# Two transformer blocks on one core: a rounding and split ahead of the gate's eviction, head sums one unit later, and six products of zeros for three

## The chip, the cores and the metric

The kernel runs on one core of a Trainium2 chip. The metric is the device time of one execution in microseconds (us), as the median of several runs. TensorE multiplies (its weight loads are listed apart, as PEld), VectorE (DVE) and ScalarE (ACT) do the element-wise work, GpSimd (POOL) helps, and SyncE (SP) issues the transfers. The engines run side by side, each takes its instructions in order, and they wait for each other by semaphores.

## The reference, cut to what matters

One token sequence of T = 256 positions with D = 1024 features, float32, runs through a first model of two layers ("stage a0", "a1"), and then through a second model of two layers ("b0", "b1"). A layer of the first model is, cut short:

```
xn   = rms_norm(h); proj = xn @ w_in            # q k v, index, conv, recurrence z, three gates
y_a  = attention over the top 64 keys; y_b = short conv * gate
y_c  = rwkv7(z):  kk = k*k_k;  kk *= rsqrt(sum over a head of kk*kk)      # "head sums of the keys"
       y = scan over time(...)
       yn = (y-mean)*rsqrt(var+eps)*ln_w + ln_b   # group norm, per head
       y_c = (yn + bonus) * g
mixed = sum over the three branches of sigmoid(gate_i) * (y_i @ w_branch_i)
h += mixed @ w_out;  h += conv_glu_ffn(rms_norm(h))
```

All products of activations with the large weights must have more than the accuracy of one rounded product, which is why each weight and each activation is split in two parts (below). The group norm and the head sums are the places that the change touches.

## The kernel before, in words

**Slabs and units.** The weights stream in as slabs of 128 x 2048 float32 (1 MB), one per unit of work; `UNITS_A` (line 44) lists the units of a layer of the first model in order. Those named here are w 0 and w 1 (the first two), rz 0 to 6 (the recurrence's inputs), uc, cb (convolution), ga, gb, gc 0 to 3 (the gates of the three branches), br0, br1, br2 (the branches' projections), out, up and down. Every unit makes three products for each weight tile (`gemm`, lines 1488 to 1490): high weight by high input, high by low, low by high. Before a unit can run, ScalarE must round its slab into `w_high` (step "round", `act_round`, line 594) and VectorE must subtract to get `w_low` (step "split", `dve_split`, line 967). There are three slab buffers and three pairs of high and low parts. A round waits for the slab's transfer and for the products of the unit three back; SyncE's next transfer into a slab waits for its split.

**Order of the work.** A list of steps is built once per stage by `schedule_a` and `woven`, and every engine walks the same list in order and does its own part of each step (`walk`). `woven` puts at unit u the round and split of the unit two ahead, then a "begin" (the first half of the unit's products) with the steps that stand amid the unit, then the unit's remaining products and its eviction, and then the steps put after it. A unit in `late` gets its round and split after the eviction instead. So the order of two steps in the list is their order in each engine's queue; an engine that has no part in a step passes over it.

**The group norm.** For gc 2 the list of before reads: begin, gn 1, unit, round and split of br2 0, gn 2. In gn 1 TensorE sums the squares per head (`head_sums`, line 1890), ScalarE takes the root (line 921, recorded like all calls of its helper under line 670) and VectorE the reciprocal (1369). In the unit ScalarE waits for the products of gc 2 and applies two sigmoids from the bank (767, also recorded under 670); they need another activation table than the root, so a table load of ScalarE lies between. In gn 2 TensorE spreads the reciprocal over the features (1901) and makes the factor g (2049); VectorE scales, adds and multiplies in two halves (1374, 1380, 1383), ScalarE makes the high part, and VectorE the low part (1101). Unit br2 0 multiplies these parts; it follows gc 3.

**The head sums of the keys.** After rz 3 GpSimd makes kk (2106), after rz 4 ScalarE squares it (864), after rz 5 TensorE sums per head (`kk_sum`, 1906, products at 1890) and VectorE clamps the sum (1287), and after rz 6 ScalarE takes the root (868) and the first attention scores are made (TensorE 1829, VectorE 1248, ScalarE exponentials 815). The sums' bank is read by the clamp only; the root is used again three units on.

**The start.** `pe_warm` multiplies zeros into a bank that nothing reads, as soon as GpSimd has set them, while the first transfers run. A product of float32 operands appears as two records of 128 x 512. TensorE's first real work is w 0 (24 products, lines 1776 to 1778), in whose first half two halves of slab 0 are waited for (`split_half`, line 978).

Of the kernel before, what the change touches and what calls it, by code (L numbers as in the profile page):

```python
# [355 lines left out]
def lead_steps(first):  # L356

    halves = [[("scaled", 2 * n), ("scaled", 2 * n + 1)] for n in range(2)]
    if first:
        steps = [("angles", 0)]  # L360
        for n in range(2):
            steps += [("scaled", n), ("round_half", n), ("split_half", n)]
        return (steps + [("angles", 1), ("angles", 2)] + halves[1] + [("round", 1), ("split", 1)]
                + [("square", i) for i in range(4)] + [("root_table", 0), ("gather", 0)])
    steps = []
    for n in range(2):
        steps += [("add", 2 * n), ("add", 2 * n + 1)] + halves[n] + [("square", 2 * n), ("square", 2 * n + 1)]
    return steps + [("gather", 0), ("split", 1)]


def woven(units, first, lead, after, mid, last=False, early=(), late=()):


    steps, rounded, n, done = list(lead), 2, len(units), set()

    def ready(u):
        nonlocal rounded
        out = []
        if rounded == u:
            out.append(("round", u))  # L380
            rounded += 1
        if u not in done:
            out.append(("split", u))
        done.add(u)
        return out

    for u in range(n):
        ahead = u + PARTS - 1
        split_next = ready(ahead) if ahead < n + (not last) else [] if last else [("round", ahead)]
        if units[u] not in late:  # L390
            steps += split_next
        if units[u] in mid:
            steps += [("begin", u)] + mid[units[u]]
        if units[u] in early:
            steps.append(("round", rounded))
            rounded += 1
        steps.append(("unit", u))
        if units[u] in late:
            steps += split_next
        for step in after.get(units[u], []):  # L400
            if step == ROUND_NEXT:
                if rounded < n:
                    steps.append(("round", rounded))
                    rounded += 1
            elif step == SPLIT_NEXT:
                steps.append(("split", u + PARTS))
                done.add(u + PARTS)
            else:
                steps.append(step)
    return steps  # L410


def schedule_a(first):
    after, mid = {}, {}

    def put(unit, *steps):
        after.setdefault(unit, []).extend(steps)

    def amid(unit, *steps):
        mid.setdefault(unit, []).extend(steps)  # L420

    amid(("w", 1), ("sum", 0), ("norm", 0), ("tables", 0))
    put(("w", 1), ("norm_x", 0))
    put(("ki", 0), ("params", 0), ("highs", 0), ("lows", 0))
    amid(("q", 0), ("ki_turn", 0))
    put(("q", 1), ("turns", 0), ("turns", 1))
    amid(("rz", 0), ("isc", 0), ("isc", 1))
    amid(("rz", 1), ("isc", 2), ("isc", 3))
    put(("rz", 2), ("turns", 2), ("turns", 3))
    for part in range(4):  # L430
        put(("rz", 1 + part), ("topk", part))
    put(("rz", 3), ("kk", 0))
    put(("rz", 4), ("kk_square", 0))
    put(("rz", 5), ("kk_sum", 0))
    put(("rz", 6), ("kk_root", 0))
    hosts = [("rz", 6)] + [("uc", i) for i in range(4)] + [("cb", 0), ("cb", 1)]
    for n, unit in enumerate(hosts):
        put(unit, *([("conv", n - 1)] if 1 <= n < 5 else []), *([("lora_inputs", 0)] if n == 2 else []))
        work = [(name, n - lag) for name, lag in (("pv", 3), ("turn", 2), ("scores", 0)) if 0 <= n - lag < 4]
        put(unit, *(work + [ROUND_NEXT] if unit == ("uc", 3) else [ROUND_NEXT] + work))  # L440
    amid(("uc", 3), ("lora", 0), ("kk_inverse", 0))
    put(("uc", 3), ("kk_spread", 0), ("kk_scale", 0), ("blend", 0), ("decay", 0), ("blended", 0))
    put(("cb", 0), ("keys", 0))
    put(("ga", 0), ("chunk", 0), ("mask", 0), ("chunk", 1), ("mask", 1))
    put(("ga", 1), ("chunk", 2), ("mask", 2), ("chunk", 3), ("mask", 3), ("blocks_out", 0), ("tok", 0), ("keys", 1), ("clear", 0),
        ("blocks_turn", 0))
    put(("ga", 2), ("invert", 0), ("tok", 1), ("post", 0), ("post", 1))
    put(("ga", 3), ("tok", 2))
    put(("gb", 0), ("off_diag", 0), ("bonus_shift", 0))
    put(("gb", 2), ("blocks_in", 0))  # L450
    put(("gb", 3), ("solve", 0))
    amid(("br0", 0), ("solve", 1))
    put(("br0", 0), ("solve", 2))
    amid(("br0", 1), ("solve", 3))
    put(("br0", 1), ("scan_rhs", 0))
    for c, unit in enumerate((("br1", 0), ("br1", 1), ("gc", 0), ("gc", 1))):
        amid(unit, ("scan_sa", c))
        put(unit, ("scan_y", c), *([("scan_rhs", c + 1)] if c < NCH - 1 else [("gn", 0), ("root_table", 0)]))
    amid(("gc", 2), ("gn", 1))
    put(("gc", 2), ("gn", 2))  # L460
    amid(("br2", 1), ("mix", 0))
    for i in range(4):
        if i < 3:
            amid(("out", i + 1), ("x_ffn", i))
            put(("out", i + 1), ("square", 4 + i))
    put(("out", 3), ("gather", 1), ("x_ffn", 3), ("square", 7), ("sum", 1))
    amid(("up", 0), ("sum", 2), ("norm", 1))
    put(("up", 0), ("spread", 1))
    put(("up", FT - 1), ("ffn", FT), ("ffn", FT + 1))
    put(("down", FT // 2 - 2), ("root_table", 0))  # L470
    return woven(UNITS_A, first, lead_steps(first), after, mid, early=[("br2", 0), ("br2", 1)],
                 late=[("gc", 2), ("br2", 1)])


def schedule_b(first):
# [38 lines left out]
    put(("out", 1), ("merge", 3))  # L514
    put(("out", 2), ("root_table", 0))
    return woven(UNITS_B, False, lead_steps(False), after, mid, not first)


SCHEDULE = {"a0": schedule_a(True), "a1": schedule_a(False), "b0": schedule_b(True), "b1": schedule_b(False)}


# [122 lines left out]
def flat(core, at, n=1):  # L644
    return core.ar[:, at * T:(at + n) * T]
# [1412 lines left out]
def pe_warm(core, eng):  # L2058

    eng.wait_ge(*core.sem("idle_set").next(eng))  # L2060
    for _ in range(3):
        eng.matmul(core.bank[6][:], flat(core, IDLE_)[:, 0:P], flat(core, IDLE_, 2), start=True, stop=True, skip_group_check=True)


def tensor_program(core, eng):
    banks = Banks(core, eng)
    pe_warm(core, eng)
    for stage in STAGES[:-1]:
        core.enter(stage)
        (tensor_a if stage[0] == "a" else tensor_b)(core, eng, banks, stage)  # L2070
    core.enter("end")
    add_up = pe_square(core, eng, banks, 4)
    for i in (1, 3, 2):
        add_up(i)
    pe_spread(core, eng, banks, "final_norm", 4)
# [855 lines left out]
```

How the kernel before makes its waits and increments, by code:

```python
    def at_least(self, eng, n):  # L117
        if n > 0:
            eng.wait_ge(self.sem, self.base + n)
# [14 lines left out]
    def settled(self):  # L134
        if self.last:
            self.eng.wait_ge(*self.last)
# [403 lines left out]
def sync_program(core, eng):  # L540
# [1 line left out]
    eng.dma_start(core.gains[:], d["gains"]).then_inc(sem("gains_in").sem, 16)  # L542
    for i in range(4):
        eng.dma_start(core.h[:, 2 * i:2 * i + 2, :], d["x_t"][:, 2 * i:2 * i + 2, :]).then_inc(sem(f"x_in{i}").sem, 16)
    slab_to(core, eng, 1)
    eng.dma_start(core.cc[:], d["common"]).then_inc(sem("const_in").sem, 16)
    slab_to(core, eng, 2)
    eng.dma_start(core.cm[:], d["const_a"]).then_inc(sem("model_in").sem, 16)
    eng.dma_start(core.vec[:], d["vec_a"][0]).then_inc(sem("vec_in").sem, 16)
    eng.dma_start(core.lora[:], d["lora"][0]).then_inc(sem("lora_in").sem, 16)
    for u in range(SLABS, SLABS_IN_ALL):
        eng.wait_ge(sem("slab_split").sem, u - SLABS + 1)
        slab_to(core, eng, u)
        if u == FIRST_SLAB["a1"] + SLABS:
            for name in ("convolved", "g_made"):
                eng.wait_ge(sem(name).sem, START["a1"][name])
            eng.dma_start(core.vec[:], d["vec_a"][1]).then_inc(sem("vec_in").sem, 16)
            eng.dma_start(core.lora[:], d["lora"][1]).then_inc(sem("lora_in").sem, 16)
        if u == FIRST_SLAB["b0"] - 20:
            eng.dma_start(core.cb[:], d["const_b"]).then_inc(sem("const_b_in").sem, 16)
    eng.wait_ge(sem("slab_split").sem, SLABS_IN_ALL)
    for i in range(4):
```

## Time and profile before

| | |
|---|---|
| median of 3 runs | 1680.03 us (1679.94 to 1680.36) |
| profiled execution | 1679.88 us, span 1678.1 us |
| TensorE busy | 1660.4 us, 99% of the span |
| weight loads | 1478.3 us, 88% |
| VectorE busy | 1196.9 us, 71% |
| ScalarE busy | 964.0 us, 57% |
| GpSimd busy | 211.7 us, 13% |
| transfers | 268.17 MB, mean 160 GB/s |
| granted TensorE clock, mean | 0.996 of full speed |

The span runs from the first to the last instruction, and the execution's time is 1.8 us longer. Busy time of TensorE counts overlapping products once, and the end of a product is modelled; so a pause shows best from the start of one product to the start of the next. A wait in the lists stands as "who <- what released it". Where the releaser is not seen it is written "issue".

### The profile page before, as it was taken

To read this page: it belongs to the slowest core of one execution; us is meant where nothing else is said; L and a number is where in the kernel's file an instruction comes from. 1 tells how busy PE (TensorE), PEld (TensorE's weight loads), DVE (VectorE), ACT (ScalarE), POOL (GpSimd) and SP (SyncE) were. 2 spreads that over 40 slices of the span, in tenths; PEclk is the share of its full clock that TensorE was granted. 3 is DMA by queue.
4 is the path that set the end of the run, shared out by engine and by line. 5 is a ranking of instruction groups with operands and counts; after the bars stand their busy time and mean duration, and the time that the engine had idled before them with its cause. 6 is when DMAs were issued, how large, how long until landed. Compare 5 with 4: busy or idle time off the path is not lost.

```text
span 1678.1 us, 29746 instructions
## 1 busy us (share of the span) xinstructions
PE 1660.4 (99%) x12378; PEld 1478.3 (88%) x12378; DVE 1196.9 (71%) x1676; ACT 964.0 (57%) x1459; POOL 211.7 (13%) x208
## 2 busy tenths in 40 slices
PE   8999999999999999999999999999999999999998
PEld 6999999999998999999999998778888987788887
DVE  7877446798888975538898875767766647667664
ACT  7674424655567564335555555665774556657743
POOL 1764400000001945200000000000000100000000
PEclk9999999999999999999999999999999999999999
DMA  7443522544545424424455454344344453443451
GB/s 266 147 152 119 178 102 101 201 179 176 185 179 184 173 101 142 155 102 175 152 183 199 176 201 176 129 148 174 128 175 177 169 199 135 150 162 141 163 188 51
DMA packets 48197, 268.17 MB, mean 160 GB/s; under 512 B 13568, under 2 KB 14464, under 8 KB 16448
## 3 DMA queue, kind: packets, MB, share of 16 engines
q1 hardware_dynamic: 38160, 263.65, 43.7%
q10 hardware_dynamic: 9136, 1.58, 0.5%
q8 instruction: 98, 1.61, 0.4%
q0 software_dynamic: 768, 1.05, 0.3%
q14 instruction: 35, 0.29, 0.0%
HBM read 264.42 MB, written 1.84 MB: 159 GB/s over the span
## 4 chain that ended last, share of the span: by engine, by line
PE 94%; DVE 3%; ACT 2%; issue 1%; DMA 0%; DVEq 0%; SPq 0%; ACTq 0%
PE bank L1488 12%; PE bank L1489 11%; PE bank L1490 11%; PE bank L2647 11%; PE bank L2649 10%; PE bank L2648 10%; PE bank L1541 8%; PE bank L1543 4%; PE bank L2677 2%; PE bank L2665 1%; DVE w_low L967 1%; PE bank L1937 1%; PE bank L1776 1%; ACT w_high L594 1%; PE bank L1778 1%; PE bank L1777 1%
## 5 line engine op out<-in xcount | busy, mean ns | idle before, releaser
L967 DVE TENSOR_TENSOR w_low<-slab,w_high 128x2048 fp32r<-128x2048 f32 x249 | 579.9, 2338 | 207.0 <-ACT w_high L594 199.7
L594 ACT ACTIVATE w_high<-slab 128x2048 fp32r<-128x2048 f32 x249 | 470.2, 1895 | 139.6 <-PE bank L2649 97.2
L1488 PE MATMUL bank<-act,w_high 128*128 128x256 f32 (+1 forms) x1744 | 503.1, 288 | 5.8 <-DVE act L1101 4.4
L1489 PE MATMUL bank<-act,w_high 128*128 128x256 f32 (+1 forms) x1744 | 493.9, 283 | 0.0
L1490 PE MATMUL bank<-act,w_low 128*128 128x256 f32 (+1 forms) x1744 | 493.7, 283 | 0.0
L1488 PEld LDWEIGHTS bank<-act,w_high 128*128 128x128 f32 (+1 forms) x1744 | 333.4, 191 | 17.1 <-issue 11.2
L1489 PEld LDWEIGHTS bank<-act,w_high 128*128 128x128 f32 (+1 forms) x1744 | 333.7, 191 | 0.9 <-issue 0.5
L1490 PEld LDWEIGHTS bank<-act,w_low 128*128 128x128 f32 (+1 forms) x1744 | 333.7, 191 | 0.1
L2647 PE MATMUL bank<-w_high,act 128*128 128x512 f32 x768 | 305.3, 398 | 0.0
L2649 PE MATMUL bank<-w_low,act 128*128 128x512 f32 x768 | 299.8, 390 | 0.0
L2648 PE MATMUL bank<-w_high,act 128*128 128x512 f32 x768 | 299.1, 389 | 0.0
L1541 PE MATMUL bank<-act,w_high 128*128 128x512 f32 x576 | 204.4, 399 | 0.0
L2202 POOL TENSOR_TENSOR arena<-arena 128x512 f32<-128x512 f32 x8 | 14.4, 1797 | 1297.7 <-ACT arena L619 1297.7
L2649 PEld LDWEIGHTS bank<-w_low,act 128*128 128x128 f32 x768 | 144.1, 188 | 31.0
L2647 PEld LDWEIGHTS bank<-w_high,act 128*128 128x128 f32 x768 | 144.3, 188 | 29.4 <-issue 1.3
L2648 PEld LDWEIGHTS bank<-w_high,act 128*128 128x128 f32 x768 | 144.5, 188 | 28.2
L670 ACT ACTIVATE arena<-bank 128x512 f32<-128x512 f32 (+3 forms) x134 | 70.1, 535 | 162.0 <-PE bank L1543 44.8
L1543 PE MATMUL bank<-act,w_low 128*128 128x256 f32 x576 | 161.8, 281 | 0.0
L1541 PEld LDWEIGHTS bank<-act,w_high 128*128 128x128 f32 x576 | 108.3, 188 | 26.1
L1543 PEld LDWEIGHTS bank<-act,w_low 128*128 128x128 f32 x576 | 108.9, 189 | 0.0
L2275 ACT ACTIVATE arena<-bank,small 128x512 f32<-128x512 f32 x80 | 54.8, 685 | 79.9 <-PE bank L2649 78.8
L1137 DVE SCALAR_TENSOR_TENSOR arena<-arena,vectors 128x255 f32<-128x255 f32 (+1 forms) x176 | 85.1, 483 | 12.4 <-ACT arena L670 3.6
(261 smaller groups left out, 1853.8 us busy)
## 6 DMA issues: line engine op xcount, KB each, us to landing
slab<-stream_a SPq DMA_DIRECT2D x143, 1024.0 KB, 4.8
slab<-stream_b SPq DMA_DIRECT2D x104, 1024.0 KB, 4.8
residual<-x_t SPq DMA_DIRECT2D x4, 256.0 KB, 6.0
slab<-stream_a ACTq DMA_DIRECT2D x2, 512.0 KB, 5.6
lora_weights<-lora SPq DMA_DIRECT2D x2, 512.0 KB, 7.7
out_t<-residual SPq DMA_DIRECT2D x4, 256.0 KB, 2.3
d_inverse<-arena POOLq DMA_DIRECT2D x2, 256.0 KB, 3.4
constants<-common SPq DMA_DIRECT2D x1, 384.0 KB, 8.8
```

The costliest lines, as they stand in the source:

```text
L594: line.did(eng.activation(core.wh[u % PARTS][:, 0:SLAB_WIDTH[u]], core.slab[u % SLABS][:, 0:SLAB_WIDTH[u]], ACT.Copy), core.sem("slab_high"))
L670: line.did(eng.activation(out, in_, func, **kw), tally)
L967: line.did(line.eng.tensor_tensor(core.wl[u % PARTS][:, 0:SLAB_WIDTH[u]], core.slab[u % SLABS][:, 0:SLAB_WIDTH[u]], core.wh[u % PARTS][:, ...
L1137: did(stt(out=out[:, lag:T], in0=src[:, 0:T - lag], scalar=col("conv", 2 * FT * tap + half * FT + j), in1=out[:, lag:T], op0=ALU.mult, op1 ...
L1488: eng.matmul(out, wh, xh, start=first, stop=False, skip_group_check=True)
L1489: eng.matmul(out, wh, xl, start=False, stop=False, skip_group_check=True)
L1490: return eng.matmul(out, wl, xh, start=False, stop=last, skip_group_check=True)
L1541: eng.matmul(out[:].rearrange("p (n t) -> p n t", n=2), wh[:, k, j, :], core.x[:, :, at, :], start=k == 0, stop=False, skip_group_check=True)
L1543: return eng.matmul(out[:, 0:T], wl[:, k, j, :], core.xh[:, at, :], start=False, stop=k == 7, skip_group_check=True)
L2647: mm(bank[b][:], high, wh[:, k, :], start=(half == 0 and k == 0), stop=False, skip_group_check=True)
L2648: mm(bank[b][:], low, wh[:, k, :], start=False, stop=False, skip_group_check=True)
L2649: last = mm(bank[b][:], high, wl[:, k, :], start=False, stop=(half == 1 and k == 3), skip_group_check=True)
```

## The change

Three edits. In `woven`, a unit named in `behind_mid` gets the round and split of the unit two ahead behind the steps amid it and ahead of its own eviction; gc 2 is named there and is in `late` no more. So at gc 2 the list reads: begin, gn 1, round and split of br2 0, unit, gn 2. The step `kk_sum` moves from behind rz 5 to behind rz 6, ahead of `kk_root`. `pe_warm` makes six products in place of three. Both layers of the first model have the first two edits; the third is at the start of the kernel alone.

```diff
-def woven(units, first, lead, after, mid, last=False, early=(), late=()):
+def woven(units, first, lead, after, mid, last=False, early=(), late=(), behind_mid=()):
...
-        if units[u] not in late:
+        if units[u] not in late and units[u] not in behind_mid:
             steps += split_next
         if units[u] in mid:
             steps += [("begin", u)] + mid[units[u]]
+        if units[u] in behind_mid:
+            steps += split_next
...
-    put(("rz", 5), ("kk_sum", 0))
-    put(("rz", 6), ("kk_root", 0))
+    put(("rz", 6), ("kk_sum", 0), ("kk_root", 0))
...
     return woven(UNITS_A, first, lead_steps(first), after, mid, early=[("br2", 0), ("br2", 1)],
-                 late=[("gc", 2), ("br2", 1)])
+                 late=[("br2", 1)], behind_mid=[("gc", 2)])
...
-    for _ in range(3):
+    for _ in range(6):
         eng.matmul(core.bank[6][:], flat(core, IDLE_)[:, 0:P], flat(core, IDLE_, 2), start=True, stop=True, skip_group_check=True)
```

## Rows read from the trace of the kernel before

**Rows 1.** The page: the chain that ended last, shares of the span by engine.

```profile
PE 94%; DVE 3%; ACT 2%; issue 1%; DMA 0%; DVEq 0%; SPq 0%; ACTq 0%
```

**Rows 2.** Waits of the whole span, TensorE only: total us, times, longest us.

```profile
PE bank L1488 <- DVE act L1101: 4.4, 2, 2.2
...
PE bank L1890 <- issue: 1.0, 2, 0.5
```

**Rows 3.** Timeline of TensorE, layer 0: start us, us, engine line op; idle time in brackets.

```profile
271.57 0.28 PE L1489 MATMUL bank<-act,w_high 128*128 128x256 f32 x1
271.69 0.28 PE L1490 MATMUL bank<-act,w_low 128*128 128x256 f32 x1
274.16 0.36 PE L1488 MATMUL bank<-act,w_high 128*128 128x256 f32 x1 [2.19 <-DVE act L1101]
```

**Rows 4.** Timeline of ScalarE, layer 0, around the group norm.

```profile
260.87 1.28 ACT L670 ACT_TABLE_LOAD   x1 [0.16 <-ACT arena L670]
263.27 0.84 ACT L670 ACTIVATE arena<-bank,vectors 128x256 f32<-128x256 f32 x2 [1.12 <-PE bank L1490]
264.00 1.91 ACT L594 ACTIVATE w_high<-slab 128x2048 fp32r<-128x2048 f32 x1
```

**Rows 5.** Timeline of VectorE, layer 0, around the group norm.

```profile
260.79 1.75 DVE L1369 RECIPROCAL arena<-arena 128x256 f32<-128x256 f32 x1 [8.16 <-ACTq L141]
265.94 2.29 DVE L967 TENSOR_TENSOR w_low<-slab,w_high 128x2048 fp32r<-128x2048 f32 x1 [3.40 <-ACT w_high L594]
268.15 0.68 DVE L1374 TENSOR_TENSOR arena<-bank,arena 128x512 f32<-128x512 f32 x1
...
273.32 1.30 DVE L1101 TENSOR_TENSOR act<-arena,act 128x512 fp32r<-128x512 f32 x2
```

**Rows 6.** Timeline of TensorE, layer 0, head sums of the keys.

```profile
76.97 0.28 PE L1490 MATMUL bank<-act,w_low 128*128 128x256 f32 x1
77.77 0.64 PE L1890 MATMUL bank<-arena,constants_a 128*32 128x256 f32 x8 [0.52 <-issue]
78.33 0.38 PE L1488 MATMUL bank<-act,w_high 128*128 128x256 f32 x1
```

**Rows 7.** Timeline of TensorE, layer 0, eight like products, for the group norm (L1890).

```profile
259.32 0.28 PE L1490 MATMUL bank<-act,w_low 128*128 128x256 f32 x1
...
260.10 0.38 PE L1488 MATMUL bank<-act,w_high 128*128 128x256 f32 x1
```

**Rows 8.** Timeline of ScalarE, layer 0, from the square of the keys on.

```profile
76.61 1.06 ACT L670 ACTIVATE arena<-arena 128x1024 f32<-128x1024 f32 x1 [4.47 <-POOL arena L2106]
...
87.11 1.28 ACT L670 ACT_TABLE_LOAD   x1
88.84 0.40 ACT L670 ACTIVATE arena<-arena,small 128x128 f32<-128x128 f32 x1 [0.44 <-DVE small L1254]
```

**Rows 9.** Timeline of VectorE, layer 0, same stretch.

```profile
83.31 0.41 DVE L1287 TENSOR_SCALAR arena<-bank 128x256 f32<-128x256 f32 x1
...
86.54 0.96 DVE L1248 SCALAR_TENSOR_TENSOR arena<-bank,arena 128x768 f32<-128x768 f32 x1
```

**Rows 10.** Timeline of TensorE, layer 0, first transpose of scores.

```profile
97.79 0.82 PE L1841 MATMUL bank<-constants,arena 128*128 128x128 f32 x6
```

**Rows 11.** Timeline of all engines, start of the kernel.

```profile
1.32 4.87 PE L2062 MATMUL bank<-arena 128*128 128x512 f32 x6 [1.32 <-POOL arena L2211]
...
8.84 0.80 PE L1776 MATMUL bank<-w_high,act 128*128 128x512 f32 x1 [2.65 <-DVE w_low L978]
...
14.26 2.29 DVE L967 TENSOR_TENSOR w_low<-slab,w_high 128x2048 fp32r<-128x2048 f32 x1 [0.85 <-ACT w_high L594]
...
16.60 0.50 PE L1776 MATMUL bank<-w_high,act 128*128 128x512 f32 x1 [0.45 <-DVE w_low L967]
```

**Rows 12.** Busy time by stretch: PE, PEld, DVE, ACT, POOL; granted clock, DMA share, GB/s.

```profile
271.00:274.00 3.00, 0.97 (x9) 0.76 (x7) 2.71 (x6) 1.08 (x3) 0.00 (x0) 1.00 0.49 208
8.84:12.35 3.51, 3.51 (x9) 2.80 (x9) 3.36 (x17) 3.48 (x8) 0.00 (x0) 0.51 0.99 407
```


## The prediction

> **What bounds the kernel now.** I read the page's chain of waits first, then the waits of TensorE alone, then the timelines of the three places that the change touches, engine by engine. The chain lies on TensorE for 94% of the span [rows 1], so an edit pays only where TensorE itself stops or does less. The list of its waits has two entries in places that are touched: 4.4 us in two stops ahead of products of L1488, released by L1101 on VectorE, and 1.0 us in two stops at L1890 [rows 2]. There are two layers, hence two stops of each; the longest of either is half its total, so the layers are alike and I work layer 0 and double it.
>
> **The first stop: the branch of the recurrence.** Inside a unit the products start 0.12 us apart (271.57, 271.69); then the next starts at 274.16 [rows 3]. Start to start that is 2.47 us, less the ordinary 0.12: TensorE loses 2.35 us. It has finished gc 3 and wants the first product of br2 0, whose input is the low part of the group norm's output, written by L1101. Back along VectorE: L1101 starts at 273.32 at the end of a row of operations that starts at 268.15 (L1374), and that starts where the split of br2 0's slab ends (it starts at 265.94) [rows 5]. The split waits for ScalarE's rounding, 264.00 to 265.91, and the rounding stands behind the sigmoids of gc 2, which wait for gc 2's products until 263.27 [rows 4]. So ScalarE idles after its root, except for a table load at 260.87, and everything behind pays for the order of two steps.
>
> **Part 1, rounding and split ahead of gc 2's eviction.** Nothing is added or removed; one rounding and one split per layer come earlier. On ScalarE the rounding starts at about 260.87, where the table load stands now: it takes 1.91 us and ends at 262.78. The load goes behind it, since it belongs to the sigmoid and stands right ahead of it: after the keys' root there is a rounding and then the load, 87.11, and then the exponentials [rows 8]. Load 1.28, so the sigmoids run from 264.06 to 264.90 in place of 263.27 to 264.11 [rows 4]: 0.8 us late. Who waits for them is the second of the two banks that br2 0 fills, at 271.8, seven us later, and the gate's product with that branch, later still: no cost. The slab that is rounded must be there and its buffer free: the buffer's last user is gc 1, finished before gc 2 began, and SyncE's transfer into the slab was released by the split of gc 1, two splits ahead of the one before this (each unit splits two ahead, and a unit with its scan takes some ten us): no queue is held.
> On VectorE the order doesn't change at all: reciprocal (260.79 to 262.54), split, group norm. The split starts at 262.81 in place of 265.94, that is 3.13 us earlier, and ends at 265.10. L1374 can follow at 265.02, since the spread of the root that it multiplies by is on TensorE right behind gc 2's products (they end near 263.2, as ScalarE's 263.27 shows [rows 4]), about one us of work. Everything up to L1101 moves with it, and so does the release of br2 0: 274.16 - 3.13 = 271.03 [rows 3, 5]. TensorE wants it at 271.81. The stop is gone with 0.78 us to spare, and the gain is the full 2.35, not 3.13. Twice: **4.70 us**. What is late next is TensorE's own work. Bounds per layer: at most 2.47 (start to start); at the low end, were only part of the shift to arrive, 3.13 - 1.28 = 1.85 (the table load ahead of the rounding after all). Below nothing only if the late sigmoids were waited for, which the seven us exclude.
>
> **Part 2, head sums of the keys one unit later.** Between the last product of rz 5 and the first of rz 6 lie 1.36 us (76.97 to 78.33) with eight records of L1890 in them [rows 6]. The same eight for the group norm, with inputs ready, take 0.78 (259.32 to 260.10) [rows 7]. The difference, 0.58 us, is a wait, though the list puts it under "issue": the square of the keys on ScalarE runs from 76.61 to 77.67, and L1890 starts at 77.77 [rows 6, 8]. One unit (over five us) later the square is long there, so the wait goes and the 0.78 stays. Twice 0.58: **1.16 us**. The sums now stand beside the attention scores, also 32 bit products; a change of kind of operand may drop out, at most the 0.14 by which the 0.78 exceed their busy 0.64 [rows 6, 7], taken as 0.
> What is queued behind: on VectorE the clamp (L1287, 0.41 us) and a split change places, both inside 83.31 to 86.54, and the scores' scaling at 86.54 stays where it is [rows 9]. On ScalarE the root of the keys waits for that clamp, so it slips from 84.88 to some 86.5, and behind it queue a rounding, the table load and the exponentials of the first pair: 86.5 + 0.4 + 1.9 + 1.28 gives 90.0 where 88.84 stood [rows 8], 1.2 us late, ending near 92. The first transpose that reads them is at 97.79 [rows 10], or 97.2 with TensorE ahead: five us of cover. The rounding ends at 88.7, as the split that waits for it wants to start, and serves a unit two further on. If the cover were gone the price would be at most 1.2 a layer, so this part lies between -1.16 -0.28 and +1.24 in all.
>
> **Part 3, six products of zeros.** Now three products are six records and 4.87 us, from 1.32 to 6.19; TensorE then idles 2.65 us until 8.84, and runs its first 3.5 us of real work at a granted clock of 0.51 [rows 11, 12], the low one of its two levels (1.2 GHz). A record at low level costs at most 4.87/6 = 0.81 us on average; the sixth came out shorter. Three more products are six more records: 2.4 us if at high level (half of 0.81), 4.9 at low, so the zeros end at 8.6 to 11.1. In the first case TensorE has hardly a pause and starts real work at 8.84 at the high level. Nine products then take some 2.1 us in place of 3.51 and the first unit ends 1.4 us or more before it does now. But it already waits 0.45 us at 16.60 for the split of slab 1 (14.26 to 16.55), which follows ScalarE's rounding, which follows the transfers and the scaling of x, and nothing in that row reads a product [rows 11]. The gain is eaten there: **0**. In the other case the first product starts 2.3 us late, less the 0.45 of slack: +1.8 is the upper bound, and 0 the lower. I take 0, since the sixth record shows the level already rising.
>
> **Sum.** Against the profiled execution, 1679.88 us (span 1678.1): 4.70 + 1.16 + 0 = 5.86 us less, 1674.0. Its own time stands 0.15 under the median of the runs shown, so 1680.03 - 5.86 = **1674.2 us**. Both gains lie in the first two layers; after them TensorE, ScalarE and VectorE are all released by TensorE's products and move together, so I let nothing be given back: the entries of TensorE's list that remain are short.
>
> **The rivals.**
> 1. The table load stays ahead of the rounding in part 1. For it: that is its place today, at 260.87. Against: with another step in between, as after the keys' root, it comes last [rows 4, 8]. The release moves 1.85, so 0.50 remains of each stop: 1675.2.
> 2. The late root of the keys costs TensorE what part 2 gives. For it: ScalarE really slips by 1.2 us at the head of the attention. Against: five us of cover [rows 8, 10]. Without part 2: 1675.4; with the whole 1.2 a layer charged on top of the gain of part 1 and 2, 1676.6.
> 3. The clock falls in the pause ahead of 16.60, which grows to about 1.8 us. For it: it did fall after the 2.65 us pause [rows 11, 12]. Against: through a stop of 2.35 us, at 271 to 274, the granted clock was 1.00 [rows 12]. One low stretch such as 8.84 to 12.35 costs 3.51 - 2.1 = 1.4 us: 1675.6. The Trainium skill ("TensorE: Matmul & The Clock Gate", section "HAM oscillation: how this bites in real kernels") says that pauses between bursts take the granted rate back, again and again if they recur, which is this rival; it would make the time that of this rival, and the pause at the start agrees with it while the stop at 271 does not.
> 4. The first stop only moves: br2 1 or the output projection waits for splits in its place, which today are done in its shadow. Against: those splits come 2.8 to 3.1 us earlier too, as they follow the same row of ScalarE. All of 4.70 lost: 1678.9, no change by the bound below.
> 5. Slower: the zeros run wholly at the low level, and the level is then not granted before the end of the second unit. Place: the 24 products of w 0 and 24 of w 1. Price: first product at 11.1, then 48 products at 0.39 (3.51/9 [rows 12]) in place of 0.23 or so; w 0 ends at 20.5, 3.9 past the wait at 16.60, and w 1 adds 24 x 0.16 = 3.8; with one more unit at that pace another 3.8. From the point where the low level outlasts 5.86 us of cost, midway through w 1, the kernel is slower: at the end of the third unit 1674.2 + 11.5 = 1685.7. Against: today the level is up at 12.35, after nine products.
> That a part doesn't do what it says is in 1, 2 and 4.
>
> **Chances.** Forecast 0.70; rival 1 0.07; rival 2 0.07; rival 3 0.06; rival 4 0.06; rival 5 0.04. About 0.2% (3.4 us) is what a measurement of this kernel can tell from no change. Forecast and rivals 1 to 3 are faster by more than that: 0.90; rival 4 is the same, 0.06; rival 5 slower, 0.04. The forecast alone: 1673.5 (2.47 a stop and both change-overs saved, 1673.7, and 0.2 for the spread of the runs) to 1674.8 (the 4.4 + 1.0 of TensorE's list in place of my gaps [rows 2], 1674.6, and the same 0.2). The range takes in rivals 1 to 3 and the price of late zeros: 1673.2 to 1676.6.
>
> **What would show it.** Right: no stop on L1488 released by L1101, br2 0 starting 0.1 to 0.2 us after gc 3's last product; the rounding directly behind the root and then the table load; L1890 in its 0.78 us just ahead of L1829 and the first exponentials near 1.2 us late with no wait of the transposes; the granted clock at 1.00 from 8.84 on, and a pause of over one us ahead of the second unit. Wrong: any new entry of over 0.5 us in TensorE's waits, a second low stretch of the clock, or a gain at the start, which would mean that the row leading to 16.60 does read TensorE's work.

## The result

The changed kernel takes 1671.55 us in the median of 5 runs (1670.91 to 1672.7), against 1680.11 (1679.94 to 1680.36) in the 5 runs of the kernel before: a ratio of 0.9948, with a 95% interval of 0.9937 to 0.996. It is 8.6 us faster, where 5.86 were forecast; the time lies 1.6 us below the range. The direction held and the size did not. Line numbers of the changed kernel are one higher than before.

The profiled execution took 1672.7 us (span 1670.9), 7.2 less than the one before. Its page, chain by engine:

```profile
PE 96%; DVE 2%; ACT 1%; issue 0%; DMA 0%; DVEq 0%; SPq 0%; ACTq 0%
```

TensorE holds the chain even more than it did [rows 1]. Its waits over the whole span, all of them (who, released by whom, us in total, times, longest):

```profile
PE bank L1777 <- DVE w_low L968: 1.5, 1, 1.5
PE bank L2063 <- POOL arena L2212: 1.3, 1, 1.3
PE bank L1677 <- DVE arena L1001: 1.1, 1, 1.1
PE bank L1489 <- DVE w_low L968: 0.9, 2, 0.4
PE bank L1777 <- DVE w_low L979: 0.3, 1, 0.3
```

The 4.4 us ahead of the first product of br2 and the 1.0 us ahead of the head sums [rows 2] are gone, in both layers.

**At the group norm of layer 0**, ScalarE, the root first:

```profile
259.85 0.48 ACT L671 ACTIVATE arena<-bank,small 128x256 f32<-128x256 f32 x1 [0.58 <-PE bank L1891]
260.50 1.92 ACT L595 ACTIVATE w_high<-slab 128x2048 fp32r<-128x2048 f32 x1 [0.17 <-ACT arena L671]
262.43 1.28 ACT L671 ACT_TABLE_LOAD   x1
263.73 0.84 ACT L671 ACTIVATE arena<-bank,vectors 128x256 f32<-128x256 f32 x2
```

The rounding comes right behind the root and the table load behind the rounding, as forecast. VectorE at the same place:

```profile
260.40 1.75 DVE L1370 RECIPROCAL arena<-arena 128x256 f32<-128x256 f32 x1 [8.16 <-ACTq L141]
262.45 2.29 DVE L968 TENSOR_TENSOR w_low<-slab,w_high 128x2048 fp32r<-128x2048 f32 x1 [0.29 <-ACT w_high L595]
...
269.83 1.30 DVE L1102 TENSOR_TENSOR act<-arena,act 128x512 fp32r<-128x512 f32 x2
```

The reciprocal starts 0.39 us earlier than before and the low part of the output 3.49 earlier [rows 5]; the difference, 3.10, is the shift that the edit brings (3.13 forecast). TensorE passes from gc 3 to br2 0 without a pause, 0.12 us from start to start, where 2.47 stood [rows 3]:

```profile
271.30 0.28 PE L1491 MATMUL bank<-act,w_low 128*128 128x256 f32 x1
271.42 0.28 PE L1489 MATMUL bank<-act,w_high 128*128 128x256 f32 x1
```

**At the head sums**, TensorE, and then the place where ScalarE takes the late root:

```profile
83.11 0.28 PE L1491 MATMUL bank<-act,w_low 128*128 128x256 f32 x1
83.32 0.64 PE L1891 MATMUL bank<-arena,constants_a 128*32 128x256 f32 x8
83.89 0.93 PE L1830 MATMUL bank<-arena 64*128 64x128 f32 x8
```

```profile
87.23 0.42 ACT L671 ACTIVATE arena<-arena 128x256 f32<-128x256 f32 x1 [3.20 <-DVEq L141]
87.55 1.90 ACT L595 ACTIVATE w_high<-slab 128x2048 fp32r<-128x2048 f32 x1
89.47 1.28 ACT L671 ACT_TABLE_LOAD   x1
90.76 0.40 ACT L671 ACTIVATE arena<-arena,small 128x128 f32<-128x128 f32 x1
```

The sums wait for nothing. The first exponential is 1.9 us later than before [rows 8]; the transposes that read it start at 97.40 (97.79 in [rows 10]) and wait for nothing either.

**Where the rest came from.** I lined up the starts of TensorE's products in both traces, from the first unit on, and noted where their distance changes:

| place | us |
|---|---|
| start: x landed 0.33 later in this execution | +0.34 |
| head sums of the keys, layers 0 and 1 | -0.73, -0.77 |
| stop ahead of br2 0, layers 0 and 1 | -2.35, -2.35 |
| **behind that stop in layer 0, 275.1 to 278.5 of before** | **-1.53** |
| **ahead of the output projection in layer 1, near 782 of before** | **-0.64** |
| the last 10 us | +0.83 |
| sum | -7.20 |

The two bold rows had no term in the prediction. The first is a stretch of the low clock in the kernel before, which starts one microsecond behind the stop. A window of that trace, next to the one over the stop in [rows 12] (us; busy time of TensorE, its weight loads, VectorE, ScalarE and GpSimd with their instructions; granted clock; transfers):

```profile
275.10:278.50 3.40, 3.40 (x19) 3.40 (x18) 2.53 (x2) 3.13 (x4) 0.00 (x0) 0.50 0.00 0
```

And TensorE's timeline there:

```profile
275.06 0.39 PE L1489 MATMUL bank<-act,w_high 128*128 128x256 f32 x1
275.25 0.42 PE L1490 MATMUL bank<-act,w_low 128*128 128x256 f32 x1
275.46 0.41 PE L1488 MATMUL bank<-act,w_high 128*128 128x256 f32 x1
...
781.99 0.28 PE L1490 MATMUL bank<-act,w_low 128*128 128x256 f32 x1
782.77 0.38 PE L1488 MATMUL bank<-act,w_high 128*128 128x256 f32 x1 [0.51 <-DVE w_low L967]
```

Inside the stop the granted clock reads 1.00; behind it, with TensorE busy throughout, it is 0.50, the lower of the two levels (1.2 GHz), and products start 0.21 us apart in place of 0.12. In the changed kernel the same work runs at the high level:

```profile
272.40:275.80 3.40, 3.40 (x31) 3.40 (x30) 3.17 (x2) 2.34 (x3) 0.00 (x0) 1.00 0.14 19
```

31 products in 3.40 us, against 19. The second bold row is the wait at 782.77 in the timeline of before: the split for the output projection came late in layer 1. In the changed kernel it didn't, as VectorE moved by 3.1 us and TensorE by only 2.35. In layer 0 of before that wait did not stand at all: TensorE was already 1.5 us late there from the low stretch.

### The profile page after: what moved, and what is told of

The parts are those of the page before. It is cut to its first block, busy times and chain, and to the rows that moved or that the text cites. A ratio compares the mean times of both kernels' runs of the same rounds, so it can differ in the third digit from the quotient of the medians.

```text
span 1670.9 us, 29758 instructions
## 1 busy us (share of the span) xinstructions
PE 1660.4 (99%) x12384; PEld 1477.3 (88%) x12384; DVE 1199.1 (72%) x1676; ACT 964.2 (58%) x1459; POOL 211.5 (13%) x208
## 4 chain that ended last, share of the span: by engine, by line
PE 96%; DVE 2%; ACT 1%; issue 0%; DMA 0%; DVEq 0%; SPq 0%; ACTq 0%
PE bank L1489 13%; PE bank L1490 12%; PE bank L1491 12%; PE bank L2648 11%; PE bank L2650 10%; PE bank L2649 10%; PE bank L1542 8%; PE bank L1544 4%; PE bank L2678 2%; PE bank L2666 1%; PE bank L1938 1%; PE bank L1777 1%; PE bank L1779 1%; PE bank L1778 1%; PE bank L2697 1%; PE bank L1982 1%
```

## The experiments

My theory A: a stop of TensorE of this size costs its own length and, behind it in one layer, a low stretch of the clock worth about 1.5 us; the 0.64 is VectorE's larger advance; each edit's gain stands by itself. The rivals are that the low stretch is chance and has nothing to do with the stop, and that the surplus comes from the zeros at the start. Each kernel was run 5 times or more, beside the kernel before on the same chip.

**Only the woven change** (`gn_only`).

```diff
+        if units[u] in behind_mid:
+            steps += split_next
...
-                 late=[("gc", 2), ("br2", 1)])
+                 late=[("br2", 1)], behind_mid=[("gc", 2)])
```

> Only the rounding and split of br2 0 move ahead of the sigmoids of gc 2; head sums and the three products of zeros as before. Theory A (the stop before br2 0 costs three things: its own 2.35 us in each layer, in layer 0 also a low stretch of TensorE's clock behind it, 275.2 to 278.5 in the profile before, worth 1.5 us, and the 0.66 us wait ahead of out 1 in layer 1, because VectorE gains 3.13 us where TensorE gains 2.35): 4.70 + 1.53 + 0.64 = 6.9 us less, near 1673.2 us, no stop ahead of br2 0, no low clock between the first unit and the tail. Rival B (the prediction's: only the stop itself goes): 4.7 less, 1675.4. Rival C (what the prediction missed came from the zeros at the start): as B.

Measured: 1673.11 us against 1680.21, ratio 0.9956 (0.9943 to 0.9968). That is 7.1 us for this edit alone, where the prediction had 4.70. Windows behind the place of the stop, layers 0 and 1:

```profile
272.40:275.80 3.40, 3.40 (x30) 3.40 (x30) 2.29 (x1) 3.39 (x4) 0.00 (x0) 1.00 0.00 0
760.00:763.40 3.40, 3.40 (x31) 3.40 (x30) 3.17 (x2) 2.38 (x3) 0.00 (x0) 1.00 0.10 17
```

With the stops gone the low stretch is gone, with the zeros and the head sums as before. The surplus belongs to this edit. This execution had a longer low stretch at its start than the kernel before, which is taken up below with the zeros; it made the execution slower, not faster.

**Only the head sums** (`kk_only`).

```diff
-    put(("rz", 5), ("kk_sum", 0))
-    put(("rz", 6), ("kk_root", 0))
+    put(("rz", 6), ("kk_sum", 0), ("kk_root", 0))
```

> Only the head sums of the keys move one unit on. Theory A: 0.58 us of wait and 0.15 us of change-over between kinds of operand go in each layer, 1.5 us less in all, near 1678.6 us; the stop ahead of br2 0 (2.35 us, twice) and the low clock behind the one in layer 0 stay. Rival: the root of the keys, 1.2 us late on ScalarE, is waited for by the transposes: no gain, 1680.1.

Measured: 1678.46 against 1680.21, ratio 0.9989 (0.998 to 0.9998), 1.75 us less. The stops are as before, and a low stretch is there again, but in the other layer. Windows of this kernel:

```profile
275.10:278.50 3.40, 3.40 (x31) 3.40 (x30) 2.82 (x2) 2.84 (x4) 0.00 (x0) 1.00 0.00 0
763.60:767.00 3.40, 3.40 (x18) 3.40 (x17) 2.48 (x2) 3.18 (x4) 0.00 (x0) 0.50 0.00 0
```

Layer 1's stop ended at 762.71. So the stretch follows a stop, but not every stop is followed by one in a given execution. The wait ahead of the output projection has changed layers too. It now stands in layer 0, where TensorE was not held up by a low stretch, and not in layer 1:

```profile
292.01 0.39 PE L1487 MATMUL bank<-act,w_high 128*128 128x256 f32 x1 [0.50 <-DVE w_low L966]
```

So a low stretch costs 1.5 us where it stands and saves the 0.6 of that wait, and the two layers have changed roles. Lined up with the kernel before, this execution gains 0.76 and 0.77 us at the two head sums and, apart from its start and its last 10 us, nothing else.

**Only the zeros** (`warm_only`).

```diff
-    for _ in range(3):
+    for _ in range(6):
```

> Only the zeros: six products in place of three. Theory A: the first unit runs at the high level of the clock and ends 1 us or so earlier, but the second still starts near 16.6 with the split of its slab, so nothing is gained: 1680.1 within 0.4. Rival C (the 2.6 us that the change gave beyond the prediction come from here, through the clock later on): 1677.5.

Measured: 1680.17 against 1680.21, ratio 0.9999 (0.999 to 1.0008): nothing. The stops are there as before. The first work runs at the high level, and what that brings is waited away ahead of the second unit:

```profile
PE bank L1776 <- DVE w_low L967: 1.5, 1, 1.5
```

The low stretch fell behind the stop of layer 1 here too:

```profile
764.90:768.30 3.40, 3.40 (x18) 3.40 (x18) 2.56 (x2) 3.10 (x4) 0.00 (x0) 0.50 0.00 0
8.84:12.35 3.51, 3.51 (x14) 2.35 (x13) 3.36 (x18) 3.48 (x7) 0.00 (x0) 1.00 0.99 408
```

**The kernel before, with its stop filled by work** (`fill_stop`): 18 products on operands that are ready, into a bank that is free. They gain no time by themselves; only the pause is gone.

```diff
+        if rows[u][0:2] == ("br2", 0):
...
+            for n in range(18):
+                eng.matmul(bank[5][:, 0:T], spare[:, P * (n % 16):][:, 0:P], core.xh[:, 8 + n % 8, :], ...)
```

> The kernel before, with 18 products of 128x256 on operands that lie ready, written to a bank that nobody reads at that time, ahead of br2 0 in both layers: the stop stays as long as it was, but TensorE works through it (18 x 0.12 = 2.2 us). It leaves nothing out. Theory A (the clock falls because TensorE pauses there): the granted clock stays at 1.00 at 275 to 278.5 and layer 0 runs 1.5 us faster from there, of which up to 0.64 comes back as a wait ahead of out 1, as layer 1 has it: 1678.6 to 1679.2 us. Rival D (the low stretch has another cause): 1680.1, clock low at 275 as before.

Measured: 1679.72 against 1680.21, ratio 0.9995 (0.9987 to 1.0004). Its timeline, and the window behind:

```profile
271.64 0.28 PE L1490 MATMUL bank<-act,w_low 128*128 128x256 f32 x1
271.76 2.32 PE L1734 MATMUL bank<-act,w_high 128*128 128x256 f32 x18
274.11 0.36 PE L1488 MATMUL bank<-act,w_high 128*128 128x256 f32 x1
...
292.24 0.39 PE L1488 MATMUL bank<-act,w_high 128*128 128x256 f32 x1 [0.51 <-DVE w_low L967]
```

```profile
274.50:278.00 3.50, 3.50 (x31) 3.50 (x30) 2.36 (x2) 3.50 (x4) 0.00 (x0) 1.00 0.00 0
```

Its clock was 1.00 from 12.3 to 1671.2 us, with no low stretch in either layer: the mechanism of A. A wait of 0.51 us appears at 292.24, ahead of the output projection in layer 0: TensorE came earlier, VectorE's split did not. Theory A had counted it in. Lined up with the kernel before, this execution gains 1.47 us in the stretch behind the stop of layer 0 and gives 0.59 back at that wait, 0.88 in all, as A says. The median time is nevertheless 0.5 us above A's range and only 0.5 below the kernel before. Part of this lies outside the span: these eleven executions take 1.9 to 2.7 us more than their spans, those of every other kernel 1.8 or 1.9, for a reason that was not found. By spans the medians are 1677.8 against 1678.4. By the interval the time of this run is no proof; its trace is the evidence. The spread of single runs is a hint. Of the 27 runs of the kernel before in this comparison, nine have a mean clock of 0.994 and take 1680.96 to 1681.74 us, the other eighteen 0.996 or more and 1679.35 to 1680.86. The eleven runs of this kernel have 0.996 or 0.997, and none takes more than 1680.17. It is no more than a hint, as the low level at the start and at the end of the kernel also moves single runs (below).

**The changed kernel, with the stop put back** (`pause_back`): two more reciprocals on VectorE, of which nothing reads the result, ahead of the low part.

```diff
+            for _ in range(2):
+                line.settled()
+                did(eng.reciprocal(flat(core, CL_), flat(core, RT_)))
             for b in range(2):
```

> The changed kernel with two reciprocals more on VectorE (1.75 us each, on a tile that is done with) ahead of L1102, the low part that br2 0 waits for. The computation is whole; the two only repeat a value. The release of br2 0 moves from 271.0 to 274.6 by the prediction's times and the stop is back, 2.8 us a layer. Theory A: two stops, 5.5 us, and one low stretch of the clock behind one of them (either layer), 1.3 to 1.5 us, since TensorE pauses longer than in the kernel before: 1678.4 to 1678.7, a low stretch in the profile behind one of the stops, perhaps two. Rival B (a stop costs its length only): 1677.1, clock high.

Measured: 1678.63 against 1680.17, ratio 0.9994 (0.9985 to 1.0002): 7.0 us slower than the changed kernel (1671.62 below). Its waits; VectorE's row of layer 0 and TensorE's of layer 1; the window behind:

```profile
PE bank L1492 <- DVE act L1102: 5.0, 2, 2.5
```

```profile
269.47 3.54 DVE L1388 RECIPROCAL arena<-arena 128x256 f32<-128x256 f32 x2
...
762.26 0.36 PE L1492 MATMUL bank<-act,w_high 128*128 128x256 f32 x1 [2.48 <-DVE act L1102]
...
764.02 0.41 PE L1492 MATMUL bank<-act,w_high 128*128 128x256 f32 x1
```

```profile
763.40:766.80 3.40, 3.40 (x19) 3.40 (x18) 3.40 (x2) 0.00 (x0) 0.00 (x0) 0.50 0.26 46
```

Lined up with the changed kernel, its products fall behind by 2.6 us in layer 0, 2.7 in layer 1, and 1.54 more in the low stretch: 6.85 in all. A stop alone brings the low stretch back, with head sums and zeros as in the change. It began 1.2 us after the stop ended at 762.26. Its eleven runs fall in two groups as well: four at a mean clock of 0.995 take 1680.34 to 1680.89, seven at 0.997 or 0.998 take 1677.91 to 1678.71.

**The changed kernel again** (`after_again`), no edit.

> The changed kernel once more, beside the next three. Theory A: 1671.6 us within 0.8; no low clock between the first unit and the tail, whatever the time at which the level is checked falls, so the runs differ only at the start and in the tail (the 24 products of one column, 2.81 us at the high level, 3.57 where the level falls among them). Rival D (the missing stretch of low clock was chance): a low stretch somewhere after 20 us, and a time 1.5 us longer.

Measured: 1671.62 against 1679.82, ratio 0.9951 (0.9939 to 0.9964). Again no low stretch up to 1664.5 us.

**The change without the zeros** (`gn_kk`): six products back to three.

> The change without its third part: three products of zeros. Theory A: the zeros give nothing, so as the changed kernel within 0.4 us: 1671.6. Rival: the zeros give what one low stretch less at the start is worth, 1.4 us: 1673.0.

Measured: 1672.0 against 1679.82, ratio 0.9953 (0.9939 to 0.9967). The runs (1671.09 to 1672.23) overlap with those of the changed kernel. In this execution the clock is low for 3.4 us at the start and it costs nothing there. The second unit starts 0.18 us earlier than in the first profile of the change, and x landed 0.17 earlier:

```profile
8.60:12.00 3.40, 3.00 (x7) 2.43 (x8) 3.25 (x17) 3.37 (x6) 0.00 (x0) 0.50 0.99 411
```

```profile
16.76 0.50 PE L1777 MATMUL bank<-w_high,act 128*128 128x512 f32 x1 [0.63 <-DVE w_low L968]
```

Not every execution with three products is like this one. In that of `gn_only` the low level lasted 6.8 us, and TensorE was still at work on the first unit when the split was ready. Its second unit started at 17.40 without a wait, 0.46 later than in the first profile of the change (16.94), with x landed at the same time:

```profile
8.00:14.80 6.80, 5.63 (x13) 4.46 (x14) 5.81 (x21) 6.77 (x11) 0.00 (x0) 0.50 1.04 416
```

Of the seven profiled executions with three products, four had 3.4 us of the low level around the first unit and three had 6.8; the six with six products had none there.

**Can the start be made to pay?** The zeros leave a wait of 1.46 us ahead of the second unit, on a row of ScalarE in which a table load and a sine stand. Two ways to take them out of it, each with six and with three products of zeros. First, the angles behind the first split (`angles_late`, `angles_late_3`):

```diff
-        return (steps + [("angles", 1), ("angles", 2)] + halves[1] + [("round", 1), ("split", 1)]
-                + [("square", i) for i in range(4)] + [("root_table", 0), ("gather", 0)])
+        return (steps + halves[1] + [("round", 1), ("split", 1)]
+                + [("square", i) for i in range(4)] + [("angles", 1), ("angles", 2), ("root_table", 0), ("gather", 0)])
```

> The changed kernel with ScalarE's sine (table load 1.28 us and 0.24 us) and VectorE's tables behind the rounding and split of slab 1 and the squares, in place of ahead of them. Theory A (the second unit waits for ScalarE's row, not for TensorE): the split of slab 1 ends 1.4 us earlier, so w 1 starts near 15.5 in place of 16.94, and the six products of zeros now pay, since w 0 ends near 15.3. Gain 1.0 to 1.4 us on the changed kernel, near 1670.4. Rival: the root of the mean square, now behind two table loads, becomes what is waited for, and the gain is lost: 1671.6.

> As the run before it, with three products of zeros. Theory A: TensorE runs w 0 partly at the low level and ends it near 16.3, so w 1 starts there and not at 15.5: 0.3 to 0.6 us less than the changed kernel, near 1671.2, and 0.8 more than with six products. Rival (the zeros are worth nothing even here): same time as with six.

Measured: 1671.52 against 1679.82, ratio 0.995 (0.9938 to 0.9963), and with three products 1672.01, 0.9952 (0.9939 to 0.9964). Timeline of the first, ScalarE and then TensorE:

```profile
11.56 1.92 ACT L595 ACTIVATE w_high<-slab 128x2048 fp32r<-128x2048 f32 x1 [0.82 <-DMA slab<-stream_a]
...
15.86 0.50 PE L1777 MATMUL bank<-w_high,act 128*128 128x512 f32 x1 [0.95 <-DVE w_low L968]
23.88 0.70 PE L1677 MATMUL bank<-arena,constants 128*128 128x256 f32 x2 [0.45 <-DVE arena L1001]
```

The second unit starts 1.08 us earlier than in the first profile of the change (16.94), but x landed 0.58 earlier in this execution, so the new order brought 0.5. The rounding now waits for the slab's transfer, and the steps that were put off are late at 23.88: the 0.5 is given back there. Second, the sine's table loaded first of all (`sine_first`, `sine_first_3`):

```diff
-        steps = [("angles", 0)]
+        steps = [("angles", 0), ("angles", 1)]
...
-    line.did(eng.activation(core.small[:, 6:7], core.small[:, 0:1], ACT.Copy))
+    line.did(eng.activation(core.small[:, 6:7], core.small[:, 0:1], ACT.Sin))
```

> The changed kernel with the sine's table loaded by ScalarE's very first operation (a sine in place of a copy of one spare column) and the sine itself ahead of the scaling of x, where ScalarE waits for x anyway. Theory A (the second unit waits for ScalarE's row): the table load of 1.28 us and the sine go from the row, the rounding of slab 1 starts when the slab has landed, near 11.5 in place of 12.66, and w 1 near 15.9 in place of 16.94; VectorE's tables are not late, so nothing is given back: 0.8 to 1.1 us less than the changed kernel, near 1670.7. Rival: something else holds the square sum or the reciprocal, gain lost, 1671.6.

> As the run before it, with three products of zeros. Theory A: TensorE, partly at the low level, ends w 0 near 16.3 and is now itself the bound: w 1 starts there, 0.4 us or so later than with six products: 1671.1. Rival (the zeros are worth nothing): as with six.

Measured: 1671.58 against 1680.17, ratio 0.9946 (0.9934 to 0.9959), and with three 1671.81, 0.9949 (0.9935 to 0.9962). No table load is left ahead of the first full rounding, which again waits for the transfer:

```profile
12.14 1.92 ACT L595 ACTIVATE w_high<-slab 128x2048 fp32r<-128x2048 f32 x1 [0.85 <-DMA slab<-stream_a]
```

Its second unit starts at 16.44, 0.60 us earlier than in the changed kernel counted from the landing of x. At 792 us a wait for GpSimd (L1628, idle for 0.16) takes 0.28 of it back, and what is left is within the scatter of the medians. Both ways the slab's transfer ends only 0.5 to 0.6 us ahead of the place where the table load let the rounding start, so no more than that was to be had, against the 1.0 to 1.4 that I expected. The two kernels with three products were profiled in executions with 6.8 us of the low level, and counted from the landing of x their second units start 1.2 us (`angles_late_3`) and 1.0 us (`sine_first_3`) later than with six. By the medians the zeros are worth 0.5 and 0.2 us here, which the runs can't tell from nothing. None of the four can be told from the changed kernel, and nothing that I ran beats it.

## Why the prediction fell short

**Part 1, the mechanism right, the size wrong.** Each step of it stands in the traces: the rounding before the table load, sigmoids 0.85 us late (0.8 forecast) and waited for by nobody, a shift of 3.10 on VectorE (3.13), no stop. The term was 4.70 and the edit alone brought 7.1. The step that failed is "The gain is the full 2.35, not 3.13": I valued the stop at its length. The stop had a second price, paid after it: 3.4 us at half the clock, 1.53 us. `fill_stop` took the pause away, and the stretch went; `pause_back` brought the pause and got the stretch. Chance is not a likely rival: the four profiled executions with the two stops (before, `kk_only`, `warm_only`, `pause_back`) have exactly one such stretch each, and the nine without have none between 16 and 1661 us. Which of the two layers pays differs (layer 0 in the kernel before, layer 1 in `kk_only`, `warm_only` and `pause_back`).

I had argued against just this in rival 3: "through a stop of 2.35 us, at 271 to 274, the granted clock was 1.00 [rows 12]". The row is true and the inference false: the window ended where the stop ended, and the clock fell 0.9 us after that. The Trainium skill, which I cited there ("TensorE: Matmul & The Clock Gate", section "HAM oscillation: how this bites in real kernels"), says that pauses between bursts take the granted rate back. I wrote that the stop at 271 did not agree with it; it does, at 275.1 to 278.5. The pauses of the page's example are waits of 3 to 5 us and the burst behind them starts slow; here 2.2 us of idle time were enough, and the burst ran at the high level for 0.9 us first.

**"I let nothing be given back: the entries that remain are short."** The entries moved the other way. The 0.78 us that VectorE gained beyond the stop, which I called "to spare", were worth 0.64 ahead of the output projection in layer 1, a wait that stood in TensorE's list of before with 1.4 us in three entries and now has 0.9 in two. With 1.53 this makes 2.2 of the 2.4 us by which `gn_only` exceeds its term. The two prices belong together. `kk_only`, `warm_only` and `fill_stop` show the wait of 0.6 in each layer in which no low stretch stands, so a low stretch by itself costs 0.9 net; the edit, which takes the stops away and moves VectorE as well, was paid both.

**Part 2, right, a little small.** 0.58 a layer was forecast, 0.73 and 0.77 came. Alone the edit brought 1.75 in the medians and 1.53 by the starts of the products, with 1.16 forecast and 1.16 + 0.28 as the upper bound, so it came out above the bound. The 0.15 and 0.19 beyond the wait agree with the 0.14 for a change of kind of operand that I took as 0; no run takes that price by itself. ScalarE's delay was larger than forecast, the first exponential 1.9 later by the clock of the trace and not 1.2. The clamp went behind both splits, to 86.72, and held back the scores' scaling, which I had let stay where it was: TensorE's cover of five microseconds took that in.

**Part 3, right within what the runs can tell.** The pairs of kernels differ by 0.04 and 0.38 us (1680.17 to 1680.21; 1671.62 to 1672.0 with overlapping runs). What I missed is that the low level at the start is not always the 3.4 us of my rows: where it lasts 6.8, the second unit starts 0.46 later (`gn_only`), and with six products such a stretch stood in none of six profiled executions. The twelve records took 7.79 us and first work began at 9.16 at the high level; the second unit still waited for its split. Its wait grew from 0.45 to 1.46; the fall of the clock that rival 3 saw in a longer pause there did not come.

**The other rivals.** The table load behind the rounding rules out rival 1, the transposes without a wait rule out rival 2, and nothing moved to br2 1 (rival 4). Rival 5 did not come: the zeros did not run wholly at the low level in any profile.

**The sum.** By medians of single edits: 7.1 + 1.75 + 0.04 = 8.9, for 8.6 measured. The edits add up, within the scatter of the medians.

**What stays open.** Why the stretch follows one stop and not the other was not found; the two stops of a kernel are alike to 0.05 us. Nor was it shown which low stretches make up the second group of runs of the kernel before, as only one execution of a kernel is profiled: a second stop with a stretch, 6.8 us of the low level at the start, and the fall in the last 10 us would each lower the mean clock. And `fill_stop` shows the clock in its trace, but its time alone does not separate the theories.

## What to carry to other kernels

A pause of an engine whose clock is granted by its load must be priced with what comes behind it: read the clock, or the distance from one product's start to the next, for several microseconds past the pause and in every repetition, before valuing the pause at its length. A slow stretch of one engine also hides the next wait on another, so its net price is less than what it costs in place (0.9 for 1.5 us here). Where removing a wait moves the feeding engine by more than the fed one, look down the list for later waits on that same feeder; they shrink too. And a faster start is worth nothing while the second unit's input is set by another row, here by a transfer that stands right behind the table load.

## What the runs showed of the hardware

A pause of 2.2 to 2.5 us of TensorE (the idle time in the lists) was followed, in one of a kernel's two layers, by 3.4 us at a granted clock of 0.50 although TensorE was busy again; this cost 1.53 and 1.54 us in the two cases measured by starts, 0.6 of it regained in the kernels with a pause of 2.2 us from a wait that then did not come. It began 0.9 us after the end of the pause in the three kernels with 2.2 us and 1.2 us after it in the one with 2.5. With the pause filled by 18 products it did not come.

The clock also fell once with no pause ahead of it. At the end of the kernel 24 products of one column run back to back, with full weight loads. The clock fell in their midst in the first profile of the change, and not in the kernel before, nor in the second profile of the change. One execution doesn't show that these products were the cause:

```profile
1659.75 3.57 PE L1628 MATMUL bank<-constants,arena 128*128 128x1 f32 x24
1664.39 1.22 PE L1677 MATMUL bank<-arena,constants 128*128 128x256 f32 x2 [1.07 <-DVE arena L1001]
```

```profile
1659.80:1663.30 3.50, 3.50 (x24) 3.44 (x24) 0.59 (x1) 2.04 (x5) 0.00 (x0) 0.76 0.00 0
```

And the second profile of the same kernel, where the clock fell later:

```profile
1659.49 2.81 PE L1628 MATMUL bank<-constants,arena 128*128 128x1 f32 x24
1663.38 0.70 PE L1677 MATMUL bank<-arena,constants 128*128 128x256 f32 x2 [1.07 <-DVE arena L1001]
```

The same work took 2.81 and 3.57 us, and the two products behind it 0.70 and 1.22. This is most of the 1.5 us between the two profiled executions of one kernel (1672.7 and 1671.16), and with the late x it is the main reason why the first profile shows only 7.2 of the 8.6 us.
